# A step of a hybrid language model on one core: retention's rotation moved into the attention, page loads and bias rows moved, four of eight value-row copies on ScalarE

## The reference

```python
q, k, v, iq, ik, iw, rq, rk, rv, rg = split(rmsnorm(x) @ w_in)      # 8 heads of 64; retention: 4 heads, 64 / 128
# indexer: score = sum_h iw_h * relu(iq_h . ik); the samples' old ik lie in pages of a cache, found by a page table
idx = top_k(score, 256)                                             # per query
att = softmax(q . k[idx] / 8 + rel_bias[bucket(distance)]) @ v[idx] # the samples' old k, v: pages again
# retention: rq, rk rotated (cos, sin of the position), rk / 8; chunks of 128 tokens, decay g_h per step
inner = ((rq rk^T) * decay) rv ;  cross = (rq state) * g^(n+1)
state = state * g^128 + (rk * g^(127-n))^T rv                       # the samples: one step from their own state
on = (o - mean(o)) * rsqrt(var(o) + eps)                            # per head of 128
y = concat(att, silu(rg) * on) @ w_out
```

## Time and profile before

| | us |
|---|---|
| median of 3 runs | 3693.28 |
| the profiled execution | 3683.93 |
| its span | 3682.2 |
| TensorE (PE) busy in it | 3336.1 (91%) |
| VectorE (DVE) | 1536.5 (42%) |
| ScalarE (ACT) | 1146.2 (31%) |
| GpSimd (POOL) | 1202.5 (33%) |

### The profile page before, as it was taken

One profiled execution on the slowest core, in us unless ns is written; L12 is line 12 of the kernel. 1 busy time (PEld: TensorE's weight loads), 2 busy tenths in 40 slices (PEclk: granted clock), 3 DMA queues, 4 the chain that ended last, 5 costly groups with the idle time before them and its releaser, 6 DMA issues. The chain is left out here.

```text
span 3682.2 us, 57041 instructions
## 1 busy us (share of the span) xinstructions
PE 3336.1 (91%) x20476; PEld 3106.7 (84%) x20476; DVE 1536.5 (42%) x2725; ACT 1146.2 (31%) x2096; POOL 1202.5 (33%) x855
## 2 busy tenths in 40 slices
PE   5869977984699999999999999999859999999998
PEld 5549973573599999999998888889749999999998
DVE  4489973333222121212257666666631221212122
ACT  3412211341333131213344544555431331212132
POOL 2015841222132222222345556554434322222222
PEclk9979988997799999999999999999869999999998
DMA  3018645004221111111223222222242111111111
GB/s 122 20 39 123 186 154 168 6 1 119 82 47 46 46 50 44 49 46 46 82 81 94 74 87 68 78 87 76 82 143 83 40 52 46 46 46 46 46 46 69
DMA packets 346881, 263.80 MB, mean 72 GB/s; under 512 B 56038, under 2 KB 312054, under 8 KB 345174
## 3 DMA queue, kind: packets, MB, share of 16 engines
q1 hardware_dynamic: 329110, 228.50, 21.1%
q10 hardware_dynamic: 10496, 15.81, 2.0%
q0 software_dynamic: 7168, 18.08, 1.4%
HBM read 219.43 MB, written 44.76 MB: 72 GB/s over the span
## 5 line engine op out<-in xcount | busy, mean ns | idle before, releaser
L232 POOL TENSOR_TENSOR w_low_sb<-w_loaded_sb,w_high_sb 128x1024 fp32r<-128x1024 f32 (+1 forms) x278 | 571.3, 2062 | 1647.1 <-ACT w_high_sb L224 1629.3
L250 PE MATMUL psum<-act_high_sb,w_high_sb 128*128 128x344 f32 (+1 forms) x2544 | 815.8, 321 | 23.0 <-PEq L188 17.2
L250 PE MATMUL psum<-act_high_sb,w_low_sb 128*128 128x344 f32 (+1 forms) x2544 | 813.8, 320 | 1.0 <-issue 1.0
L250 PE MATMUL psum<-act_low_sb,w_high_sb 128*128 128x344 f32 (+1 forms) x2544 | 814.0, 320 | 0.0
L250 PE MATMUL psum<-second_high_sb,w_high_sb 128*128 128x344 f32 x1728 | 553.3, 320 | 0.5 <-PEq L2173 0.5
L250 PE MATMUL psum<-second_low_sb,w_high_sb 128*128 128x344 f32 x1728 | 551.9, 319 | 0.0
L250 PE MATMUL psum<-second_high_sb,w_low_sb 128*128 128x344 f32 x1728 | 551.9, 319 | 0.0
L250 PEld LDWEIGHTS psum<-act_high_sb,w_high_sb 128*128 128x128 f32 (+1 forms) x2544 | 477.8, 188 | 25.0 <-issue 24.7
L250 PEld LDWEIGHTS psum<-act_high_sb,w_low_sb 128*128 128x128 f32 (+1 forms) x2544 | 478.3, 188 | 1.7 <-issue 1.3
L250 PEld LDWEIGHTS psum<-act_low_sb,w_high_sb 128*128 128x128 f32 (+1 forms) x2544 | 477.9, 188 | 0.4
L224 ACT CAST w_high_sb<-w_loaded_sb 128x1024 fp32r<-128x1024 f32 (+1 forms) x230 | 239.8, 1043 | 601.2 <-PE psum L250 541.0
(11 more groups left out here) (426 smaller groups left out, 4691.8 us busy)
## 6 DMA issues: line engine op xcount, KB each, us to landing
w_loaded_sb<-in_w_up SPq DMA_DIRECT2D x64, 512.0 KB, 4.1
w_loaded_sb<-in_w_down SPq DMA_DIRECT2D x64, 512.0 KB, 3.6
w_loaded_sb<-in_w_in_odd SPq DMA_DIRECT2D x48, 512.0 KB, 4.0
key_pages_sb<-in_cache_k SPq DMA_DIRECT2D x64, 256.0 KB, 2.8
ecay_sum_spread_sb<-decay_sum_scratch SPq DMA_DIRECT2D x8, 2048.0 KB
w_loaded_sb<-in_w_in_even SPq DMA_DIRECT2D x28, 512.0 KB, 3.9
x_sb<-x_scratch SPq DMA_DIRECT2D x2, 4128.0 KB, 13.9
gated_scratch<-gated_sb POOLq DMA_DIRECT2D x8, 1032.0 KB, 4.4
```

The lines of the kernel that those rows point to most:

```text
L232: ins = self.nc.gpsimd.tensor_tensor(self.wl[:, par, k, 0:width], self.wf[:, par, k, 0:width], self.wh[:, par, k, 0:width].bitcast(F32), A ...
L250: ins = nc.tensor.matmul(out, w[:, par, k, 0:width], a[:, k, cols], start=n == 0, stop=n == 3 * KT - 1)
```

## The change

- The indexer's SyncE loads only the pages of samples 0 to 3; GpSimd loads those of samples 4 to 7 after its splits and memsets. `turn_pages` waits for GpSimd's pages at its third call.
- The bias products, their store and their spreading move from keys_and_values into the indexer, in a class `BiasLine`: products behind the first projection unit, store and spreading on ScalarE's queue. keys_and_values only loads the result.
- keys_and_values: key rows have four buffers; value rows of odd blocks are copied by ScalarE; the value store, and the waits for retention's spills, are awaited later; of the value pages ScalarE issues halves 0 to 2 and SyncE 3 and 4 (the last behind key row 5, ahead of the stores of rows 6 and 7), the attention's SyncE 5 to 15 instead of 7 to 15.
- Class `Rotary`: in the attention, after the last value page is used, SyncE loads retention's queries, keys, their swapped halves and cos, sin into room that the value pages had; VectorE does twelve operations of 128x1032, one after each of head steps 40 to 51; then SyncE loads retention's values.
- retention: no rotation; the samples' block is merged into the first (states loaded at its start, the diagonal in chunk 2); weight casts after chunk 0, the gates' Silu one head at a time after chunks 1 to 4, GpSimd's weight splits before chunk 2.
- Normalisation: all Ln before all Exp, squares one head ahead; the gates are multiplied before the deviation is known; two of four low parts on VectorE.

The diff, cut to its core:

```diff
+class BiasLine:
...
+        nc.tensor.matmul(B.psum[0:HA, 6, 0:384], self.rel[:], self.buckets[:, 0:384], start=True, stop=True)
...
+        act.dma_start(self.B.bias_rows, bass.AP(tensor=self.scratch.tensor, offset=0,
+                                                ap=[[0, P], [384, HA], [1, 384]])).then_inc(self.s_line, 16)
...
+    def load_pages(eng, first, sem):
+
+        with eng.Fori(first, first + NS // 4) as c:
+            for e in range(2):
+                with eng.Fori(0, PAGES) as j:
+                    page = eng.value_load(B.pages[0:1, bass.ds(c * (2 * PAGES) + j + e * PAGES, 1)], min_val=0, max_val=NPOOL - 1)
+                    eng.dma_start(pk[:, bass.ds(c * (2 * PAGES) + j * 2 + e, 1), :],
+                                  B.i["cache_idx_k"][0][bass.ds(page, 1)].rearrange("o p d -> p o d")).then_inc(sem, 16)
+
     with nc.Block() as block:
...
+                    line.load(sp)
...
-            with sp.Fori(0, NS // 2) as c:
-                for e in range(2):
-                    with sp.Fori(0, PAGES) as j:
-                        page = sp.value_load(B.pages[0:1, bass.ds(c * (2 * PAGES) + j + e * PAGES, 1)], min_val=0, max_val=NPOOL - 1)
-                        sp.dma_start(pk[:, bass.ds(c * (2 * PAGES) + j * 2 + e, 1), :],
-                                     B.i["cache_idx_k"][0][bass.ds(page, 1)].rearrange("o p d -> p o d")).then_inc(s_page, 16)
+            load_pages(sp, 0, s_page)
...
+            pool.wait_ge(s_table, 16)
+            load_pages(pool, NS // 4, s_page_pool)
             for e in range(AHEAD):
...
         def _(pe):
             norm.pe(pe)
+            line.pe(pe)
             for e in range(1, 5):
...
             def turn_pages(c):
+                if c == NS // 4:
+                    pe.wait_ge(s_page_pool, 8 * NS * PAGES)
...
+                if e == 2:
+                    line.store(act)
+                if e == 4:
+                    line.spread(act)
...
-            for e in range(2):
-                act.wait_ge(s_spill[e], 16 * 6)
             act.wait_ge(smp.s_q, 64)
...
-    kn = B.take("k_rows_sb", [P, 2, 512])
...
+    kn = B.take("k_rows_sb", [P, KEPT, 512])
...
+    by_act = [n for n, (part, b) in enumerate(steps) if part == 2 and b < NBLK and b % 2 == 1]
...
-            sp.wait_ge(s_biasc, 1)
-            sp.dma_start(b_scratch, line[:]).then_inc(s_line, 16)
-            sp.wait_ge(s_line, 16)
...
-            sp.dma_start(b_rows, bass.AP(tensor=b_scratch.tensor, offset=0,
-                                         ap=[[0, P], [384, HA], [1, 384]])).then_inc(s_line, 16)
-            sp.wait_ge(s_line, 32)
-            sp.dma_start(B.bias[:], bass.AP(tensor=b_rows.tensor, offset=P - 1,
+            sp.dma_start(B.bias[:], bass.AP(tensor=B.bias_rows.tensor, offset=P - 1,
...
+            smp.load_values(sp, 3)
             for n, (part, b) in enumerate(steps):
                 if part == 1 and b < NBLK:
-                    sp.wait_ge(s_kept, n + 1)
+                    await_kept(sp, n)
+                    if b == NBLK - 2:
+                        smp.load_values(sp, 4)
                     sp.dma_start(B.o["k_prompt"][0, 0, b * P:(b + 1) * P].rearrange("p h d -> p (h d)"),
-                                 kn[:, b % 2, :]).then_inc(s_k[b % 2], 16)
-            sp.wait_ge(s_kept, len(steps))
+                                 kn[:, b % KEPT, :]).then_inc(s_k[b % KEPT], 16)
+            await_kept(sp, len(steps) - 1)
+            await_kept(sp, len(steps) - 2)
...
-            sp.wait_ge(s_v, 48)
             sp.wait_ge(s_biast, 16)
-            for e in range(2):
-                sp.wait_ge(s_k[e], 64)
+            for e in range(KEPT):
+                sp.wait_ge(s_k[e], 16 * NBLK // KEPT)
...
             for n, (part, b) in enumerate(steps):
+                if n in by_act:
+                    smp.probs_dve(dve, n)
+                    continue
...
+                    out, rows = kn[:, b % KEPT, :], P
+                    if b >= KEPT:
+                        dve.wait_ge(s_k[b % KEPT], 16 * (b // KEPT))
                 else:
+                    if b == 0:
+                        for e in range(2):
+                            dve.wait_ge(B.s_spill[e], 16 * 6)
...
-            for m in range(smp.VRING):
+            for m in range(smp.AHEAD_ACT):
                 smp.load_values(act, m)
-            smp.probs_act(act)
+            for e in range(2):
+                act.wait_ge(B.s_spill[e], 16 * 6)
+            for n in by_act:
+                if n == 14:
+                    smp.probs_act(act)
+                act.wait_ge(s_turned, n + 1)
+                nc.scalar.copy(B.vn[:, steps[n][1], :], B.psum[:, 4 + n % 4, :]).then_inc(s_kept_act, 1)
...
+class Rotary:
...
+    FROM = 5 * HA
...
+    def load(self, sp, smp):
+        B = self.B
+        sp.wait_ge(smp.s_taken, smp.HALVES)
+        sp.dma_start(self.qk, B.r_scratch[0:4].rearrange("k p c -> p k c")).then_inc(self.s_load, 16)
+        for e, name in enumerate(("cos", "sin")):
+            sp.dma_start(self.cs[:, e, :], B.i[name]).then_inc(self.s_tab, 16)
+        for a in range(4):
+            src = a ^ 1
+            sp.dma_start(self.sw[32 * a:32 * a + 32], B.r_scratch[0:4, 32 * src:32 * src + 32]
+                         .rearrange("k p c -> p k c")).then_inc(self.s_swap, 16)
+        sp.wait_ge(self.s_turn, 12)
+        sp.dma_start(self.sw, B.r_scratch[4:8].rearrange("k p c -> p k c")).then_inc(self.s_values, 16)
...
+        if m < 8:
+            x = (self.qk if m < 4 else self.sw)[:, a, :]
+            nc.vector.scalar_tensor_tensor(out=x, in0=x, scalar=scale, in1=self.cs[:, m // 4, :], op0=ALU.mult,
+                                           op1=ALU.mult).then_inc(self.s_turn, 1)
+        else:
+            dve.wait_ge(self.s_turn, 5 + a)
+            nc.vector.tensor_tensor(self.qk[:, a, :], self.qk[:, a, :], self.sw[:, a, :], ALU.add).then_inc(self.s_turn, 1)
...
-            for m in range(smp.VRING, smp.HALVES):
+            for m in range(smp.AHEAD, smp.HALVES):
                 smp.load_values(sp, m)
+            rotary.load(sp, smp)
+            sp.wait_ge(B.s_v, 48)
+            sp.wait_ge(rotary.s_values, 16)
...
+                rotary.dve(dve, n)
...
-            sp.dma_start(r[:, 0:4, :], B.r_scratch[0:4].rearrange("k p c -> p k c")).then_inc(s_load, 16)
+            for dst, name in ((kdecay, "kdecay"), (tab[:, 0:512], "decay"), (tab[:, 512:768], "qdecay"), (sdecay, "sdecay")):
+                sp.dma_start(dst, B.i[name]).then_inc(s_tab, 16)
+            for b in range(NS):
+                sp.dma_start(st[:, b], B.i["state_ret"][0, b].rearrange("(c two) k v -> (two k) c v", two=2)).then_inc(s_stl, 16)
             load_ahead(B, sp, w_next)
-            for dst, name in ((cs[:, 0, :], "cos"), (cs[:, 1, :], "sin"), (tab[:, 0:512], "decay"), (tab[:, 512:768], "qdecay"),
...
+            sp.dma_start(r[:, 8:12, :], B.r_scratch[8:12].rearrange("k p c -> p k c")).then_inc(s_rest, 16)
...
+            sp.wait_ge(s_new, 2)
+            for b in range(NS):
+                sp.dma_start(B.o["ret_sample"][0, b].rearrange("(c two) k v -> (two k) c v", two=2), st[:, b]).then_inc(s_sto, 16)
...
+                if n == 0:
+                    high_ahead(B, act)
+                if 1 <= n <= HR:
+                    act.wait_ge(s_rest, 16)
+                    nc.scalar.activation(r[:, 7 + n, :], r[:, 7 + n, :], ACT.Silu).then_inc(s_gate, 1)
...
             for n in range(NBLK):
-                if n == 0:
-                    pool.wait_ge(s_rot, 3)
+                if n == 2:
+                    low_ahead(B, pool)
                 if n >= 2:
...
-            dve.wait_ge(s_tab, 16 * 6)
-            dve.wait_ge(s_load, 16)
-            nc.vector.tensor_tensor(r[:, 0:4, :], r[:, 0:4, :], cs[:, 0, :].unsqueeze(1).to_broadcast([P, 4, TOK]),
...
-            nc.vector.tensor_tensor(r[:, 2:4, :], r[:, 2:4, :], sw[:, 2:4, :], ALU.add).then_inc(s_keys, 1)
-            nc.vector.tensor_tensor(r[:, 0:2, :], r[:, 0:2, :], sw[:, 0:2, :], ALU.add).then_inc(s_rot, 1)
...
+                if n == 2:
+                    dve.wait_ge(s_kept, NBLK + 2)
+                    nc.vector.tensor_tensor(kd, srow[:, 0:256].unsqueeze(1).to_broadcast([NS, NS, 256]),
+                                            B.ident[0:NS, 0:NS].unsqueeze(2).to_broadcast([NS, NS, 256]), ALU.mult).then_inc(s_kd2, 1)
...
                 if h >= 1:
-                    pe.wait_ge(s_rs, 2 * h - 1)
+                    pe.wait_ge(s_ln, h)
...
+                dve.wait_ge(s_oc, h + 1)
+                nc.vector.tensor_tensor(r[:, 8 + h, :], oc[:, h, :], r[:, 8 + h, :], ALU.mult).then_inc(s_og, 1)
+
+            def low(h):
+                dve.wait_ge(s_hi, h + 1)
...
             for h in range(HR):
-                dve.wait_ge(s_oc, h + 1)
-                dve.wait_ge(s_rs, 2 * h + 2)
-                nc.vector.tensor_tensor(o[:, h, :], oc[:, h, :], sq[:, h, :], ALU.mult).then_inc(s_on, 1)
```

(33 more changed lines are left out.)

198 lines of the change are left out of this document (102 added, 96 removed).

## The result

| | before | after | ratio (95% interval) |
|---|---|---|---|
| median of 4 runs, us | 3694.02 | 3606.47 | 0.9762 (0.9745 to 0.9779) |
| lowest and highest | 3690.14, 3695.38 | 3601.60, 3607.18 | |
| profiled execution | 3683.93 | 3607.18 | |
| its span | 3682.2 | 3605.6 | |

Forecast were 3583 us, from 3566 to 3604; measured is 2.5 us above the range. The medians differ by 87.5 us, the two spans by 76.6. I follow the spans stage by stage, with the instant at which each stage hands over; the column "forecast" is the prediction's term.

The account below looks back on a forecast made before the run. Before 994 us the prediction saw TensorE's holes as the bound: waits for pages, keys and values, retention, and a low clock in the samples. Gains 21 + 30 - 1 + 60 = 110 us from 3693.3 gave 3583 us, range 3566 to 3604.

Parts of the forecast that it names:

- terms 1 and 2: Indexer: pages shared by SyncE and GpSimd, 21 us gained; keys and values: shorter waits, copies on ScalarE, 30 us gained.
- Term 3: Attention: the rotation's twelve VectorE operations, 14.8 us together, were to cost 1 us, bounds 0 and 14.8.
- Term 4: Retention and its normalisation: 43.4 - 1.5 + 6 + 12, together 60 us gained.
- first part: Retention's start: parts already rotated, turnings at once, chunks 14.1 us in instead of 57.5, 43.4 us gained.
- Samples: Retention's samples: no gap before the 64 products, which run at 2.4 GHz; 6 us gained, bounds 3 and 10.
- normalisation: Retention's normalisation: all Ln before all Exp, fewer table loads, low parts shared; 12 us gained, bounds 6 and 16.
- A: Indexer: GpSimd's page issues slow beside VectorE, 4.5 us a page; its gain becomes -28, time 3632 us; 6%.
- D: Indexer: GpSimd's issues so slow, 6.8 us a page, that the kernel is slower than before, 3701 us or more; 2%.
- B: Keys and values: key stores stay behind the value pages; gain there 17 us, time 3596 us; 14%.
- C: Rotation lies on the path in full, 3597 us, or samples and sums keep the lower clock, 3592 us; 12%.
- E: Keys and values without store waits, normalisation's sums without gaps: 3570 us; 12%.

Follow-up runs that it names:

- 7: Kernel after, with all eight value rows copied by VectorE again: 3604.0 us.
- 6: Kernel after, without the rotation's twelve VectorE operations in the attention, loads kept: 3605.0 us.
- Runs 1, 2 and 3: Kernel after, GpSimd's splits behind chunk 2's and 3's queries, one each: 3582.0 us; after, 32 turnings in the pause: 3583.3; before, with a real pause: 3707.9.
- 5: Turnings added in the samples' part: 38 on the kernel with the splits apart, 3595.7 us; 45 on the 3568.3 us kernel, 3583.9 us.
- 9: All four low parts on VectorE, on the kernel with the splits apart: 3580.7 us; plus turnings in the chunks and a keys' table semaphore: 3568.3 us.
- the splits apart: Kernel after, with GpSimd's two weight splits behind the decayed queries of chunks 2 and 3, one each, instead of both ahead of chunk 2's: 3582.0 us.

## Why the prediction missed

- **What bounds, terms 1 and 2: right.** The pages were worth 20.6 (21), keys and values 28.8 (30). Inside term 2 two sizes were off against each other: the store waits fell to 2.2 instead of 5 us, and the copies on ScalarE, put at 2.8, are worth nothing (7). That the sum of term 2 fits is luck to that extent.
- **Term 3: right, and for less.** The rotation costs nothing measurable (6); the attention's clock moves the stage by more than the rotation does.
- **Term 4, first part: right.** Turnings at once, chunks 13.7 us in (14.1).
- **Term 4, the step that failed:** "GpSimd's two weight splits stand ahead of the third decayed query: -1.5", and of the samples' products "Without the gap they should find 2.4 GHz, which the chunks have". I priced the late query as a wait, without a working, and took the chunks' clock as given. The wait was 3.25 us, twice that, since VectorE's diagonal, moved to the same place by the same change, came beside GpSimd's multiplication: it fits VectorE's own wait, as I read, but GpSimd's query took 2.77 instead of 0.73 us. But the wait's price was what came behind it: at the lower clock the chunks' products last 44 us, and 20.7 us are lost instead of 1.5. Runs 1, 2 and 3 show it in three ways: without the pause, with the pause filled, and with a pause put into the other kernel. I had a rival in which the lower clock stays for samples and sums, and none in which it takes the chunks. The trace of before showed such a price in the normalisation: the same six sums take 2.00 us behind 1.68 us of rest and 3.81 behind 4.54.

```profile
967.32 2.00 PE L2085 MATMUL psum<-halves_swapped_sb,ones_sb 128*128 128x344 f32 x6 [1.68 <-ACT halves_swapped_sb L2105]
...
973.86 3.81 PE L2085 MATMUL psum<-halves_swapped_sb,ones_sb 128*128 128x344 f32 x6 [4.54 <-ACT halves_swapped_sb L2105]
```

- **Samples (3.1 of 6) and normalisation (7.9 of 12): mechanism partly right, sizes off.** The gap ahead of the outer products did go, but they lost the higher clock in every profile in which they had it (5). The normalisation had its two table loads instead of eight. By the forecast's own marks its last cast ended 33.2 us in instead of 32.3, behind a second mean at the lower clock (3.81 us where before had 2.00), and its last low part 38.0 instead of 34.2: 2.8 us are the low parts, two on either engine side by side (9).
- **The median and the profiled execution.** I set aside the 9.3 us between them as something on which nothing hung. The profile showed the kernel before near its best: 8 of 47 of its executions are 16 us and more above it, while the four runs of the kernel after lie within 5.6 us, its profiled one among them. That is why the medians gained 87.5 and the spans 76.6. The clock is the likely cause, since over whole executions it was 0.946 in the profiled one and 0.938 to 0.941 in those eight; in which stage they lose it is not shown.
- **Rivals.** A did not occur, nor D, its larger form (its limit is 6.6 us a page by its own terms, not 6.8): GpSimd takes 1.8 us a page beside VectorE's sums. The Trainium skill ("SBUF — State Buffer", A bandwidth-pool intuition that's wrong) has some 3100 ns for such a DMA beside a copy on VectorE; here the longest of 32 took 875 ns, the median 535. B did not either: 2.2 us of store waits. Of C the first half did not occur (6), the second did: the samples and the first sums had the lower clock, and their two stages fell 7.0 us short of the forecast (2.9 and 4.1, the low parts included), where C had 9. Of E the store waits nearly came true, the sums did not.

## What to carry to other kernels

A pause of TensorE has two prices, its length and the clock behind it; ask what runs next, and whether such products have ever brought the clock up in this kernel. Here turnings of 128x128 did, and the chunks' products did not in 44 us, so 3 us ahead of them cost 20. Before trusting a profile's clock column, see how far the profiled execution lies from the median: with the splits apart the chunks were at 1.00 in one profiled execution and at 0.50 in two others, and 3 of 13 executions were slow. And when two engines' moved pieces land in one place, price them together.

## What the runs showed of the hardware

- The chunks have two states at the same work: 4.63 us a chunk at clock 1.00, 7.7 at 0.50, and in no profile did they change from the lower to the higher one, while the turnings from 794.9 on did within 6 us (granted clock 0.50 until 800.1, 1.00 in the chunks). The Trainium skill ("TensorE: Matmul & The Clock Gate", What's actually happening) has the clock follow how busy TensorE is; the fall behind a pause agrees, the 44.00 busy of 44.00 us at 0.50 do not.
- The outer products with 8 rows of weights lost the clock without any pause before them (with the splits apart, 1.00 at 839.5 and 0.50 from 842.5 on), and turnings between them did not hold it (0.65 to 1.12 us for eight).
- VectorE's and GpSimd's operations on two on-chip operands hold each other up: 1.17 to 3.3 us for VectorE's low part, 0.73 to 2.77 for GpSimd's decayed query. The Trainium skill ("SBUF — State Buffer", SBUF: two separate sides) has a port pair of which one of the two engines is locked out; the rows agree.
- Ln and Exp each load a table (two rows of 1283 ns in the new order, eight before), where the Trainium skill ("ScalarE: Activation LUTs", Table sets: the hidden batching unit) knows a set with both. A Square behind an Ln loads none.
